# Blocked triangular inverse in a two-layer kernel: X updated as X times E, with the copies on ScalarE

## What is computed

```python
def second_block(x, positions, ...):
    for l in range(DEPTH):                      # DEPTH = 1
        h = rms_norm_2(x, g_mix[l])
        p = h @ w_in[l]
        y_a = mla_group(p[..., :MLA_COLS], ...)     # 8 heads of latent attention
        y_b = rwkv7_group(p[..., MLA_COLS:], ...)   # 8 heads of RWKV-7, 64 wide
        x = x + jnp.concatenate([y_a, y_b], axis=-1) @ w_o[l]
        x = x + peer_ffn(rms_norm_2(x, g_ffn[l]), ...)
    return x

def rwkv7_step(state, inp):
    r_t, w_t, k_t, v_t, kk_t, a_t = inp
    sk = jnp.einsum('bhij,bhj->bhi', state, kk_t)
    state = (state * w_t[:, :, None, :] - sk[..., None] * (kk_t * a_t)[:, :, None, :]
             + v_t[..., None] * k_t[:, :, None, :])
    y = jnp.einsum('bhij,bhj->bhi', state, r_t)
    return state, y
```

## Time and profile before

| | us |
|---|---|
| median of 3 executions | 1568.48 |
| lowest, highest | 1567.7, 1570.97 |
| the profiled execution's own time | 1568.15 |
| its span | 1566.3 |
| TensorE busy (matmuls) | 1473.1 |
| VectorE busy | 1066.3 |
| ScalarE busy | 720.9 |
| GpSimd busy | 319.3 |

### The profile page before, as it was taken

The page is one execution under the profiler, slowest core; times in us unless marked ns, Lnnn a source line. Parts: engine busy times, 40 slices in busy tenths (PEclk is TensorE's granted clock), DMA queues, the critical chain, the costliest instruction groups (busy, mean ns, idle before and its releaser), DMA issues.

```text
span 1566.3 us, 24908 instructions
## 1 busy us (share of the span) xinstructions
PE 1473.1 (94%) x10282; PEld 1319.0 (84%) x10282; DVE 1066.3 (68%) x1804; ACT 720.9 (46%) x1223; POOL 319.3 (20%) x149
## 2 busy tenths in 40 slices
PE   7999899999989687889999999999999999999998
PEld 6887688998877675778999999999998888888886
DVE  5665555665468969563599988999965555555554
ACT  4574444554344441324444455444444444444443
POOL 0046000000044431056799910000000000000000
PEclk9999999999999889869999999999999999999999
DMA  7623433555543300024565554444455566666563
GB/s 274 212 89 126 155 115 108 177 187 196 186 154 105 120 28 1 1 81 135 172 191 164 168 168 147 145 145 147 147 169 162 189 189 189 189 189 189 188 188 122
DMA packets 64881, 235.26 MB, mean 150 GB/s; under 512 B 7425, under 2 KB 7681, under 8 KB 64513
## 3 DMA queue, kind: packets, MB, share of 16 engines
q1 hardware_dynamic: 63904, 231.60, 46.0%
q10 hardware_dynamic: 864, 2.07, 0.4%
HBM read 232.60 MB, written 1.05 MB: 149 GB/s over the span
## 4 chain that ended last, share of the span: by engine, by line
PE 80%; DVE 10%; POOL 4%; ACT 2%; issue 2%; DMA 1%; ACTq 0%; DVEq 0%; POOLq 0%
PE ps L130 79%; POOL spl L145 3%; PE ps L139 1%; ACT spl L142 1%; DVE junk L145 1%; DVE spl L145 1%; DVE prep L145 1%; DVE pm L145 1%; DMA raw<-in_w_in_a 1%; DVE be L145 1%; DVE pR L145 1%; DVE pm L154 1%; DVE hx L145 1%; DMA par<-in_par 0%; POOL QK L145 0%
## 5 line engine op out<-in xcount | busy, mean ns | idle before, releaser
L130 PE MATMUL ps<-xhl,spl 128*128 128x256 f32 x4944 | 608.7, 283 | 11.1 <-POOL spl L145 9.7
L130 PEld LDWEIGHTS ps<-xhl,spl 128*128 128x128 f32 x4944 | 593.1, 189 | 14.5 <-POOL spl L145 11.3
L142 ACT ACTIVATE spl<-raw 128x1024 fp32r<-128x1024 f32 (+1 forms) x435 | 454.1, 1048 | 321.8 <-PE ps L130 303.8
L145 DVE TENSOR_TENSOR spl<-raw,spl 128x1024 fp32r<-128x1024 f32 (+1 forms) x329 | 402.2, 1228 | 222.8 <-ACT spl L142 221.1
L130 PE MATMUL ps<-spl,Wr 128*128 128x512 f32 x1536 | 358.8, 396 | 3.3 <-DVE Wr L145 3.3
L130 PEld LDWEIGHTS ps<-spl,Wr 128*128 128x128 f32 x1536 | 290.5, 189 | 71.4 <-DVE Wr L145 3.5
L145 POOL TENSOR_TENSOR spl<-raw,spl 128x1024 fp32r<-128x1024 f32 (+1 forms) x106 | 274.4, 2605 | 286.6 <-ACT spl L142 286.2
L142 ACT ACTIVATE Wr<-GE 128x256 fp32r<-128x256 f32 x128 | 53.3, 417 | 183.6 <-PE ps L130 183.6
L142 ACT ACTIVATE GE<-ps 128x256 f32<-128x256 f32 (+42 forms) x176 | 57.0, 326 | 126.5 <-DVE GE L145 109.8
L145 DVE TENSOR_TENSOR Wr<-GE,Wr 128x256 fp32r<-128x256 f32 x128 | 54.3, 425 | 81.4 <-ACT Wr L142 81.4
L130 PE MATMUL ps<-spl,ahl 128*128 128x512 f32 x384 | 90.1, 396 | 0.0
(11 more groups left out here) (337 smaller groups left out, 1241.8 us busy)
## 6 DMA issues: line engine op xcount, KB each, us to landing
raw<-in_eu SPq DMA_DIRECT2D x128, 512.0 KB, 3.5
raw<-in_ev SPq DMA_DIRECT2D x128, 512.0 KB, 4.1
raw<-in_w_up SPq DMA_DIRECT2D x32, 512.0 KB, 3.6
raw<-in_w_down SPq DMA_DIRECT2D x32, 512.0 KB, 3.5
raw<-in_w_in_a SPq DMA_DIRECT2D x16, 512.0 KB, 5.5
raw<-in_w_pq SPq DMA_DIRECT2D x16, 512.0 KB, 3.5
raw<-in_w_rwkv SPq DMA_DIRECT2D x14, 512.0 KB, 3.5
raw<-in_w_in_t SPq DMA_DIRECT2D x8, 512.0 KB, 3.5
```

Source lines behind the costliest of these rows:

```text
L130: return Done(self, self.e and self.e.matmul(out, l, r, start=st, stop=sp))
L142: return Done(self, self.e and self.e.activation(out, a, f, bias=bias, scale=scale, accum_out=acc))
L145: return Done(self, self.e and self.e.tensor_tensor(out, a, b, op))
```

## The change

Per level, E = (the mask `ex{l}`, ones on the diagonal and minus ones on this level's blocks) times ((I + L) X), and the new X is X E. For this the identity is added once to the L columns of `GB`, by two VectorE instructions of 128 x 1024, and the masks are made accordingly. VectorE's mask step stays, with the other mask and the other name (E in `QX`'s place). The second product then is the new X itself and is no longer subtracted: ScalarE copies it from the two banks into `Xc`, VectorE transposes it into `Yc`. In level 5, ScalarE and VectorE copy the product's halves for each j straight into `Y`, and the former two copies at the end go. The marks XY become X, and in level 5 Y_a and Y_v for each j. VectorE's `turns.go()` moves from ahead of its inverse step to behind it. ScalarE goes through two turns, and then has a step in each of the next two, ahead of the turn.

```diff
@@ constants
-        d[f"lx{l}"] = one(lev)[:, 0:64] + one(lev)[:, 64:128]
+        d[f"ex{l}"] = d["eye2"] - one(lev)[:, 0:64] - one(lev)[:, 64:128]
@@ tensor
-            pe.wait_ge("GB")
             for l in range(1, 6):
                 for j in range(2):
                     if l == 1:
+                        pe.wait_ge("GBi", j)
                         pe.wait_ge("X0", j)
                     else:
-                        pe.wait_ge("XY", (l - 1, j, 1))
+                        pe.wait_ge("X", (l - 1, j, 1))
...
-                        pe.give("qd", (l, 0, j, c), "QX", (l, j, c))
+                        pe.give("qd", (l, 0, j, c), "E", (l, j, c))
                 for j in range(2):
-                    pe.wait_ge("QX", (l, j, 1))
+                    pe.wait_ge("E", (l, j, 1))
...
-                        pe.give("qd", (l, 1, j, c), "XY", (l, j, c))
+                        pe.give("qd", (l, 1, j, c), *(("X", (l, j, c)) if l < 5 else (("Y_a", "Y_v")[c], j)))
@@ scalar
             for l in range(1, 6):
-                for _ in range(4):
+                for _ in range(2):
+                    turns.go()
+                for j in range(2):
+                    js = slice(8 * j, 8 * j + 8)
+                    act.wait_ge("qd_ps", (l, 1, j))
+                    if l < 5:
+                        for c, hs in enumerate(halves):
+                            act.act(Xc[hs, js, :], pv(act.ps("qd", (l, 1, j, c)), hs), ACT.Copy).then_inc("X", (l, j, c))
+                    else:
+                        act.wait_ge("Y_z")
+                        act.act(Y[0:64, js, 0:64], pv(act.ps("qd", (l, 1, j, 0)), halves[0]), ACT.Copy).then_inc("Y_a", j)
                     turns.go()
             turns.end("t")
-            for j in range(2):
-                act.wait_ge("XY", (5, j, 1))
-            act.wait_ge("Y_z")
-            act.act(Y[0:64, :, 0:64], Yc[0:64, :, :], ACT.Copy).then_inc("Y_a")
@@ vector, behind level 0
                 dve.tr(Xc[:, js, :]..., Yc[:, js, :]...).then_inc("X0", j)
+                dve.tt(GB[:, js, 0:128], GB[:, js, 0:128], bc(ident, 1, 8), ALU.add).then_inc("GBi", j)
@@ vector, levels
                 for j in range(2):
                     js = slice(8 * j, 8 * j + 8)
-                    turns.go()
                     dve.wait_ge("qd_ps", (l, 0, j))
                     dve.wait_ge("pm", 11)
                     for c, hs in enumerate(halves):
-                        dve.tt(QX[hs, js, :], ..., bc(D(f"lx{l}")[hs, :], 1, 8), ALU.mult).then_inc("QX", (l, j, c))
+                        dve.tt(QX[hs, js, :], ..., bc(D(f"ex{l}")[hs, :], 1, 8), ALU.mult).then_inc("E", (l, j, c))
+                    turns.go()
                 for j in range(2):
                     js = slice(8 * j, 8 * j + 8)
+                    if l < 5:
+                        dve.wait_ge("X", (l, j, 1))
+                        dve.tr(Yc[:, js, :]..., Xc[:, js, :]...).then_inc("Yt", (l, j))
+                    else:
+                        dve.wait_ge("qd_ps", (l, 1, j))
+                        dve.wait_ge("Y_z")
+                        dve.cp(Y[64:128, js, 64:128], pv(dve.ps("qd", (l, 1, j, 1)), halves[1])).then_inc("Y_v", j)
                     turns.go()
-                    dve.wait_ge("qd_ps", (l, 1, j))
-                    M = Xc if l < 5 else Yc
-                    dve.wait_ge("X0" if l == 1 else "Yt", j if l == 1 else (l - 1, j))
-                    for c, hs in enumerate(halves):
-                        v = dve.tt(M[hs, js, :], M[hs, js, :], pv(dve.ps("qd", (l, 1, j, c)), hs), ALU.subtract).then_inc("XY", (l, j, c))
-                    if l < 5:
-                        dve.after(v)
-                        dve.tr(Yc[:, js, :]..., Xc[:, js, :]...).then_inc("Yt", (l, j))
             turns.end("k")
-            dve.wait_ge("XY")
-            dve.wait_ge("Y_z")
-            dve.cp(Y[64:128, :, 64:128], Yc[64:128, :, :]).then_inc("Y_v")
```

More of the change, by code:

```diff
@@ L1589, in scalar @@
             turns = Turns(mla(), tokens(), iter(()))
+            pv = lambda b, hs: b[hs, :].rearrange("p (a b) -> p a b", a=8)
             for l in range(1, 6):
-                for _ in range(4):
+                for _ in range(2):
[9 more added lines that the diff above has]
+                        act.act(Y[0:64, js, 0:64], pv(act.ps("qd", (l, 1, j, 0)), halves[0]), ACT.Copy).then_inc("Y_a", j)
                     turns.go()
             turns.end("t")
-            for j in range(2):
-                act.wait_ge("XY", (5, j, 1))
-            act.wait_ge("Y_z")
-            act.act(Y[0:64, :, 0:64], Yc[0:64, :, :], ACT.Copy).then_inc("Y_a")
             for _ in range(6):
@@ L2204, in vector @@
                     for c, hs in enumerate(halves):
-                        dve.tt(QX[hs, js, :], pv(dve.ps("qd", (l, 0, j, c)), hs), bc(D(f"lx{l}")[hs, :], 1, 8), ALU.mult).then_inc("QX", (l, j, c))
+                        dve.tt(QX[hs, js, :], pv(dve.ps("qd", (l, 0, j, c)), hs), bc(D(f"ex{l}")[hs, :], 1, 8), ALU.mult).then_inc("E", (l, j, c))
+                    turns.go()
                 for j in range(2):
                     js = slice(8 * j, 8 * j + 8)
-                    turns.go()
-                    dve.wait_ge("qd_ps", (l, 1, j))
-                    M = Xc if l < 5 else Yc
-                    dve.wait_ge("X0" if l == 1 else "Yt", j if l == 1 else (l - 1, j))
-                    for c, hs in enumerate(halves):
-                        v = dve.tt(M[hs, js, :], M[hs, js, :], pv(dve.ps("qd", (l, 1, j, c)), hs), ALU.subtract).then_inc("XY", (l, j, c))
-                    if l < 5:
-                        dve.after(v)
-                        dve.tr(Yc[:, js, :].rearrange("p a b -> p (a b)"), Xc[:, js, :].rearrange("p a b -> p (a b)")).then_inc("Yt", (l, j))
+                    if l < 5:
+                        dve.wait_ge("X", (l, j, 1))
+                        dve.tr(Yc[:, js, :].rearrange("p a b -> p (a b)"), Xc[:, js, :].rearrange("p a b -> p (a b)")).then_inc("Yt", (l, j))
+                    else:
+                        dve.wait_ge("qd_ps", (l, 1, j))
+                        dve.wait_ge("Y_z")
+                        dve.cp(Y[64:128, js, 64:128], pv(dve.ps("qd", (l, 1, j, 1)), halves[1])).then_inc("Y_v", j)
+                    turns.go()
             turns.end("k")
-            dve.wait_ge("XY")
-            dve.wait_ge("Y_z")
-            dve.cp(Y[64:128, :, 64:128], Yc[64:128, :, :]).then_inc("Y_v")
             for b_ in range(2):
```

## The result

The changed kernel took 1578.08 us (median of 4 runs, 1577.24 to 1579.58), the kernel before 1568.17 (4 runs). The ratio is 1.0064, 95% interval 1.0052 to 1.0076: slower by 9.9 us. The profiled execution took 1577.24, its span is 1575.5; before it was 1568.15 and 1566.3.

What follows compares the result with a forecast made beforehand. The order of waits in one stage (565 to 635 us) was taken to bound the change, TensorE being nearly full around it. 0.8 + 5.5 + 2.3 - 2.4 = 6.2 on 1568.15 gave 1574.3; range 1567.5 to 1579.

Steps and rivals of the forecast that it cites:

- Part 2: Turns 0 to 3: small scalings wait behind a transpose needing ScalarE's X copy, so the first rotation comes later; +5.5.
- rival C: Slower still: TensorE at half clock through Part 3 (+2 more) and in MV and TAT (+1 to 2); 1578, chance 0.12.
- Part 4: Second rotation to MV: VectorE gets 7.7 less work, TensorE's 22.1 busy plus 2.6 waits remain; -2.4, bounds 0 and -5.0.
- Part 1: Identity added to GB on VectorE delays w_ukv's first piece, so TensorE's 512-wide matmuls wait; +0.8, at most 2.4.
- Part 3: First to second rotation: level 3's transpose stands ahead of the second rotation; 8.9 becomes 11.2, +2.3.
- all at half clock: Upper bound of Part 3, with TensorE at half clock throughout: 13.2 (+4.3).
- Behind MV: MV, TAT and after: no term in the sum; removing the two copies of Y gives nothing.
- Rival A: VectorE's 7.7 come back up to TensorE's bound (Part 4 -5.0), Part 1 0, Part 3 +0.4; 1569, chance 0.17.
- Rival B: Denser work after the second rotation keeps TensorE's clock high through 631 to 646 and later; 1562, chance 0.12.

Runs made afterwards that it cites:

- scalings_first: Changed kernel, but at level 1, second half, VectorE takes its turn (the two small scalings) ahead of the transpose; 1573.59 us, ratio to before 1.0034.
- rotation2_first: Changed kernel, but at level 3, first half, VectorE takes its turn (second block's rotation) ahead of the transpose; 1573.89 us, ratio to before 1.0034.
- after_clock_kept: Changed kernel plus 80 identity transposes in TensorE's idle time ahead of the first rotation's transposes; 1578.64 us, ratio to before 1.0067.
- before_idle_filled: Kernel before plus identity transposes on TensorE: 70 ahead of the first rotation's transposes, 5 ahead of the second's, 15 ahead of MV; 1564.03 us, ratio 0.9979.
- before_turns_behind: Kernel before, X still updated on VectorE, with only VectorE's turns moved behind its inverse steps; 1575.92 us, ratio to before 1.0047.

## Why the prediction was right where it was, and where it was off

I forecast 1574.3 and slower by 6.2; it is 1578.1 and slower by 9.9. The sign and the main step, Part 2, were right by their mechanism. The time lies outside the 1572 to 1577 of the forecast itself and inside the range only because the range took in rival C. Up to TAT my terms gave 5.4 and the stage 9.8; of the 4.4 between them 3.7 lie in Part 4 and behind it. Point by point:

- **Part 1 (+0.8).** Measured 0.49. The piece's low half started at 557.16, right behind the additions, which took 1.18 each.
- **Part 2 (+5.5).** Measured +5.9. The mechanism is the one in the prediction, and scalings_first takes away 4.5 of it. The size is off by the copies: I took 1.08 for a pair of 64x512 from the nearest row, they took 1.22 and 1.19, the upper bound that I had named, and two pairs stand ahead of the scalings.
- **Part 3 (+2.3).** Measured +2.6 (11.54 against 8.93). With the clock kept it is 2.3 (9.63 against 7.32). rotation2_first shows the cause. The "all at half clock" didn't come (and 13.2 was too low for it: three sets at 1.97, four groups at 1.02 and the 4.1 behind them make 14.1): the clock rose at 604.5, some 4 into the work, as before. The Trainium skill's rule on the idle gap ("TensorE: Matmul & The Clock Gate", section "HAM oscillation — how this bites in real kernels") agrees with the trace: after 13.82 idle the work started at half clock.
- **Part 4 (-2.4).** Measured -0.4, and this step failed in its size. The waits were as I had said: 0.78, 0.23 and 1.87 of idle time remain, 2.9 against my 2.6. But I held TensorE's own 22.1 for fixed. It was 23.65 in the trace. Of the 1.5 on top, 1.3 came from the second block's transposes, which ran at half clock after an idle time of 3.32 that I had myself announced. With the clock kept, the part takes 25.1 against 26.9, a gain of 1.8.
- **Behind MV (0).** I took MV and TAT as equal and gave the clock to rivals B and C. Measured +1.7: the clock fell 0.3 into MV and not 2.2 into it. The term was missing from the sum, and that it came with this size is in part chance: after_clock_kept, with the same order and the same wait ahead of it, had MV in 5.02. Of the removed copies of Y I had said that they give nothing. At the clock of the kernel before that holds; with the clock kept they were worth a wait of 0.90 (before_idle_filled).
- **Rival A** let VectorE's gain come back in full; of the 5.0 it counted on in Part 4, 0.4 came. **Rival B** had the clock rise with denser work. It didn't: in the changed kernel TensorE was busy 23.65 of 26.50 ahead of MV, before 22.11 of 27.10, and MV is slower, not faster. What decided was where the clock's fall happened to lie, with idle times of 1.82 and 1.87 ahead of MV. **Rival C**, slower still by the clock, is what came, by a fall in MV and in the second block's transposes rather than all through Part 3.
- What I said about the cause was half of it. I put the loss of Part 2 on the combination of the moved turns and ScalarE's queue. before_turns_behind shows that the moved turns cost 7.3 up to TAT in the kernel before without any copy on ScalarE, because at three places, not two, a step on which TensorE or GpSimd waits stood behind a step of the inverse for no need. At the first rotation the combination does decide: 5.9 with the copies, 1.7 without them.

## What to carry to other kernels

Where independent work is interleaved by hand in in-order queues, "step, then filler" and "filler, then step" are different kernels: a step that waits holds up all fillers behind it, and one of them may be the head of the critical chain. Before moving a call, list for each turn what stands behind the wait, and find those whose result goes to a slow engine next. And a wait ahead of TensorE can cost twice: its own length, and the clock of the work behind it. Here a wait of 3.32 did (twelve transposes in 2.77), one of 0.84 didn't (1.49). So price both, in both kernels, when an edit makes one longer.

## What the runs showed of the hardware that I had not expected

- Harmless transposes in TensorE's idle time pay: 70 + 5 + 15 of them took 3.9 us off the kernel before (0.21%, interval 0.09 to 0.34%), 120 + 28 + 15 took 8.6 off the changed one. Where the first filling left 0.85, 0.80 or 0.54 of the idle time, the clock stayed full. Where it left 5.31 or 3.80, the clock fell before the work began; where it left 3.38, it fell 0.5 into the work. None of these three changed the time by more than the runs can tell.
- A transpose of 128x128 in a long row of its kind took 0.111 (13.26 for 120), against 0.148 in a group of four (0.59 in the chain of the kernel before).
- The clock can fall while TensorE is fully busy, and full work doesn't bring it back soon: in the kernel before it fell 2.2 into MV, with 2.00 of 2.00 busy ahead of the fall and an idle time of 1.82 ahead of MV; in the changed kernel it was at 0.50 over 638.93 to 648.93, with 10.00 of 10.00 busy.
- VectorE's rotation beside GpSimd took 7.17 to 7.22 in most of the kernels, 6.70 to 6.84 where it did not start with GpSimd's next instruction; in each of these it ended some 0.6 behind GpSimd's last product.
